# Weight streams of a two-block layer: three reduced matmuls on split operands, or one plain 32-bit matmul on the landed weights

## The reference, cut to what matters

```python
# first block
u = rmsnorm(h, attn_norm_w);      z_xbc_q_k_v = u @ w_in          # 2048 x 5184
h = h + mixed @ w_out                                             # 2048 x 2048
v = rmsnorm(h, ffn_norm_w)
h = h + (silu(v @ w_gate) * (v @ w_up)) @ w_down                  # 2048 x 5632, twice; 5632 x 2048
# second block
z = rms_norm(h, g) @ w_in_2                                       # 2048 x 7176
h = h + rms_norm(y @ w_out_2, g)                                  # 2048 x 2048
u = conv3(rms_norm(h, g) @ w_up_2); gate, up = split(u)           # 2048 x 11264
h = h + rms_norm((silu(gate) * up) @ w_down_2, g)                 # 5632 x 2048
h = h + rms_norm((p @ w_ple_proj_2) * sigmoid(rms_norm(h, g) @ w_ple_gate_2), g)
```

## Time and profile before

| | |
|---|---|
| median of 3 runs | 2508.01 us (2504.28 to 2508.35) |
| the profiled execution | 2508.06 us, of which the span is 2506.3 us |
| mean granted clock of PE | 0.994 of full speed |
| busy: PE, DVE, ACT | 2473.7, 1455.4 and 1251.8 us |
| moved by the transfers | 446.27 MB, 178 GB/s over the span |

### The profile page before, as it was taken

The page is one execution under the profiler, slowest core; times in us unless marked ns, Lnnn a source line. Parts: engine busy times, 40 slices in busy tenths (PEclk is TensorE's granted clock), DMA queues, the critical chain, the costliest instruction groups (busy, mean ns, idle before and its releaser), DMA issues.

```text
span 2506.3 us, 32631 instructions
## 1 busy us (share of the span) xinstructions
PE 2473.7 (99%) x11947; PEld 2067.1 (82%) x11947; DVE 1455.4 (58%) x1732; ACT 1251.8 (50%) x1604; POOL 44.9 (2%) x103
## 2 busy tenths in 40 slices
PE   8999999999999999999999999999999999999997
PEld 7888878888888888888888888878888888888886
DVE  6479665545445454445566566566666666544465
ACT  5357744444444444444654355456556555444464
POOL 2300000000000000000000000000000000000000
PEclk9999999999999999999999999999999999999999
DMA  7543445666666666555654555555565656665554
GB/s 254 175 134 113 135 136 184 191 187 191 186 191 188 189 192 202 192 192 178 171 175 135 151 143 177 186 158 183 186 185 183 190 178 189 199 200 193 193 194 142
DMA packets 234754, 446.27 MB, mean 178 GB/s; under 512 B 14288, under 2 KB 31012, under 8 KB 234144
## 3 DMA queue, kind: packets, MB, share of 16 engines
q1 hardware_dynamic: 231920, 434.83, 56.2%
q0 software_dynamic: 2736, 10.10, 1.3%
HBM read 442.78 MB, written 2.10 MB: 178 GB/s over the span
## 4 chain that ended last, share of the span: by engine, by line
PE 96%; DVE 2%; ACT 1%; issue 0%; DMA 0%; SPq 0%; DVEq 0%; ACTq 0%
PE pg L2191 26%; PE pg L2193 26%; PE pg L2192 26%; PE pg L2250 3%; PE pg L2251 3%; PE pg L2252 3%; PE pt L2851 1%; DVE wlo L1347 1%; PE pt L2666 1%; PE pt L2262 1%; PE pt L2370 1%; PE pt L2435 1%; PE pt L2461 1%; PE pt L2448 0%; PE pt L2649 0%
## 5 line engine op out<-in xcount | busy, mean ns | idle before, releaser
L1347 DVE TENSOR_TENSOR wlo<-raw,whi 128x1024 fp32r<-128x1024 f32 (+3 forms) x844 | 1004.9, 1197 | 980.4 <-ACT whi L653 978.7
L653 ACT ACTIVATE whi<-raw 128x1024 fp32r<-128x1024 f32 (+3 forms) x844 | 871.8, 1036 | 1164.1 <-PE pg L2193 1048.5
L2191 PE MATMUL pg<-whi,AH 128*128 128x512 f32 (+1 forms) x1920 | 749.5, 390 | 5.1 <-DVE AL L1486 3.0
L2193 PE MATMUL pg<-whi,AL 128*128 128x512 f32 (+1 forms) x1920 | 742.8, 387 | 0.0
L2192 PE MATMUL pg<-wlo,AH 128*128 128x512 f32 (+1 forms) x1920 | 742.1, 387 | 0.0
L2191 PEld LDWEIGHTS pg<-whi,AH 128*128 128x128 f32 x1920 | 362.1, 189 | 77.1 <-DVE AL L1486 3.4
L2193 PEld LDWEIGHTS pg<-whi,AL 128*128 128x128 f32 x1920 | 361.6, 188 | 73.7
L2192 PEld LDWEIGHTS pg<-wlo,AH 128*128 128x128 f32 x1920 | 362.3, 189 | 70.8
L2191 PE MATMUL pg<-whi,FH 128*128 128x512 f32 x696 | 271.3, 390 | 0.0
L2193 PE MATMUL pg<-whi,FL 128*128 128x512 f32 x696 | 270.8, 389 | 0.0
L2192 PE MATMUL pg<-wlo,FH 128*128 128x512 f32 x696 | 270.8, 389 | 0.0
(11 more groups left out here) (477 smaller groups left out, 2033.1 us busy)
## 6 DMA issues: line engine op xcount, KB each, us to landing
raw<-w_up SPq DMA_DIRECT2D x264, 512.0 KB, 3.8
raw<-w_down SPq DMA_DIRECT2D x176, 512.0 KB, 3.6
raw<-w_in SPq DMA_DIRECT2D x152, 512.0 KB, 3.6
raw<-w_gate SPq DMA_DIRECT2D x88, 512.0 KB, 3.6
raw<-w_out SPq DMA_DIRECT2D x64, 512.0 KB, 3.6
raw<-w_ple_gate SPq DMA_DIRECT2D x32, 512.0 KB, 4.5
raw<-w_in SPq DMA_DIRECT2D x32, 388.0 KB, 3.2
raw<-w_in SPq DMA_DIRECT2D x16, 280.0 KB, 3.0
```

What stands on the lines that cost most here:

```text
L653: A(whi[:, n % RING, 0:w], raw[:, n % RING, 0:w], ACT.Copy).then_inc(hi_ready, 1)
L1347: V.tensor_tensor(wlo[:, n % RING, 0:w], raw[:, n % RING, 0:w], whi[:, n % RING, 0:w].bitcast(F32), ALU.subtract).then_inc(lo_ready, 1)
L2191: mm(o, xh, wh, start=first and k == 0, stop=False)
L2193: ins = mm(o, xl, wh, start=False, stop=last and k == SK - 1)
```

## The change

Each unit becomes one matmul of `F32` operands: a tile of activations `x` and the landed weights in `raw`. The rounded copies and the rests, of weights and of operands, are gone, with the semaphores between ACT and DVE that they needed. The ring `raw` has eight steps. PE waits for the landing itself, and SP for PE's `step_used` of eight steps before.

```diff
-RING = 4
+RING = 8
...
-                        sp.wait_ge(lo_ready, n - RING + 1 + d)
+                        sp.wait_ge(step_used, n - RING + 1 + d)
...
-                A(whi[:, n % RING, 0:w], raw[:, n % RING, 0:w], ACT.Copy).then_inc(hi_ready, 1)
...
-                V.tensor_tensor(wlo[:, n % RING, 0:w], raw[:, n % RING, 0:w], whi[:, n % RING, 0:w].bitcast(F32),
-                                ALU.subtract).then_inc(lo_ready, 1)
...
+            def landed(n, d=0):
+
+                pe.wait_ge(raw_landed[n % RING], 16 * (n // RING + 1) + d * (16 // RING))
...
+                landed(n, d)
                 for k in range(SK):
-                    wh = whi[:, n % RING, k * w:(k + 1) * w]
-                    wl = wlo[:, n % RING, k * w:(k + 1) * w]
                     for t in range(NT):
-                        mm(o, xh, wh, start=first and k == 0, stop=False)
-                        mm(o, xh, wl, start=False, stop=False)
-                        ins = mm(o, xl, wh, start=False, stop=last and k == SK - 1)
+                        ins = mm(pg[:, b + t, 0:w], x[:, kt0 + k, t * P:(t + 1) * P], raw[:, n % RING, k * w:(k + 1) * w],
+                                 start=first and k == 0, stop=last and k == SK - 1)
```

The activations need one copy out of `pt` now instead of a copy and a subtraction. The turned tiles come in groups of two; ACT copies the even groups and DVE the odd ones, each with the scale as before (`prep` on both engines, semaphores `even_ready` and `odd_ready`):

```diff
-                for g in (2 * c, 2 * c + 1):
-                    act.wait_ge(turned, quarters(p) + g + 1)
...
-                        ins = A(hi[:, kt - kt0, :], src[:, k, :], ACT.Copy, scale=sc)
-                    ins.then_inc(a_hi, 1)
+                g = 2 * c
+                act.wait_ge(turned, quarters(p) + g + 1)
...
+                        ins = A(dst[:, 2 * g + k - kt0, :], src[:, k, :], ACT.Copy, scale=VT[:, w:w + 1])
+                ins.then_inc(even_ready, 1)
...
+                g = 2 * c + 1
+                dve.wait_ge(turned, quarters(p) + g + 1)
...
+                        ins = V.tensor_scalar(dst[:, 2 * g + k - kt0, :], src[:, k, :], VT[:, w:w + 1], None, ALU.mult)
+                ins.then_inc(odd_ready, 1)
```

More of the change, by code:

```diff
@@ L643, in link, with stream @@
                 act.wait_ge(act_chain, chain[0])
[L645 to L652, removed]
-                A(whi[:, n % RING, 0:w], raw[:, n % RING, 0:w], ACT.Copy).then_inc(hi_ready, 1)
[L655 to L678, removed]
+            def stream(g, evac, between):
+                for c in range(len(g["chunks"])):
+                    for j in range(g["S"]):
+                        between.get((c, j), no)()
+                    evac(c, 0, g["N"] + (c + 1) * g["S"])
             def evac_copy(dst, g, scale=1.0):
@@ L1004, in down, with f1_copy @@
                         between.get((c, j), no)()
-                        split(N + c * S_ + RING + j)
                     evac(c, 0, N + (c + 1) * S_)
             F1, F2 = G["ffn1"], G["ffn2"]
-            def f1_hi(c, d):
+            def f1_copy(c, d):
                 act.wait_ge(f_turned, c + d)
-                A(FH[:, ds((d + c - 1) * 4, 4), :], pt[:, 0:2, :].rearrange("p b (c n) -> p (b c) n", n=TOK), ACT.Copy)\
-                    .then_inc(f_hi, 1)
+                A(FT[:, ds((d + c - 1) * 4, 4), :], pt[:, 0:2, :].rearrange("p b (c n) -> p (b c) n", n=TOK), ACT.Copy)\
+                    .then_inc(f_ready, 1)
             def f1_silu(c, d):
@@ L1180, in _ @@
                     evac_in1(n // 8)
-                split(RING + n)
-            f1_in = lambda c: lambda: prep(2, lambda k: V_FFN + k, AH, c)
+            f1_in = lambda c: lambda: prep(2, lambda k: V_FFN + k, XA, c)
             if upto < 8: return
@@ L1214, in _ @@
             between.update({at_step(fox_start(u) + 1): lambda u=u: fox(u) for u in range(10)})
-            stream(G["in2"], evac_copy(Z2, G["in2"], SM[:, 4:5]), between, loop=False)
+            stream(G["in2"], evac_copy(Z2, G["in2"], SM[:, 4:5]), between)
             if upto < 13: return
@@ L1220, in _ @@
                 between.get(i, no)()
-                split(G["out2"]["N"] + RING + i)
                 if i in HALF_ENDS:
@@ L1236, in _, with p_copy2 @@
             f2_in(0)()
-            split(F2["N"] + 2)
             f2_in(1)()
-            split(F2["N"] + 3)
             if upto < 17: return
-            ffn(F2, [after(f2_up), after(f2_conv_up), lambda c, d: (f2_gate(c, d), after(f2_hi)(c, d)), f2_conv_gate],
+            ffn(F2, [after(f2_up), after(f2_conv_up), f2_gate, f2_conv_gate],
                 {2: f2_in(2), 4: f2_in(3), 6: norm_ffn2})
-            def p_parts():
+            def p_copy2():
                 act.wait_ge(p_tr, 1)
-                A(PH[:], pt[:, 3, :].rearrange("p (k n) -> p k n", k=2), ACT.Copy).then_inc(p_hi, 1)
+                A(XP[:], pt[:, 3, :].rearrange("p (k n) -> p k n", k=2), ACT.Copy).then_inc(p_ready, 1)
             g = G["down2"]
@@ L1311, in _ @@
                     between.get((c, j), no)()
-                    split(g["N"] + c * 8 + RING + j)
                 if c == 0:
@@ L1339, in link, with stream @@
                 dve.wait_ge(dve_chain, chain[0])
-            def split(n, d=0, w=None):
-                if n >= NSTEP:
-                    return
-                w = SK * (w or WIDTH[n])
-                dve.wait_ge(hi_ready, n + 1 + d)
-                V.tensor_tensor(wlo[:, n % RING, 0:w], raw[:, n % RING, 0:w], whi[:, n % RING, 0:w].bitcast(F32),
-                                ALU.subtract).then_inc(lo_ready, 1)
-            def stream(g, evac, between={}, loop=True):
-                S_, N, n = g["S"], g["N"], len(g["chunks"])
-                def one(c, dc, dn):
-                    for j in range(S_):
-                        if isinstance(dc, int):
-                            between.get((c, j), no)()
-                        split(N + c * S_ + RING + j, dn)
-                    evac(c, dc, N + (c + 1) * S_ + dn)
-                for c in range(2):
-                    one(c, 0, 0)
-                loops = uniform_pairs(g)
-                if loops > 2 and loop:
-                    with dve.Fori(0, loops - 1) as i:
-                        for c in (2, 3):
-                            one(c, i * 2, i * (2 * S_))
-                    done = 2 * loops
-                else:
-                    done = 2
-                for c in range(done, n):
-                    one(c, 0, 0)
+            def stream(g, evac, between):
+                for c in range(len(g["chunks"])):
+                    for j in range(g["S"]):
+                        between.get((c, j), no)()
+                    evac(c, 0, g["N"] + (c + 1) * g["S"])
             def evac_copy(dst, g, scaled=False):
@@ L1728, in side @@
                     s = unit_step(u)
-                    if n == s + 7 and UNITS[u][0]:
-                        o_low(u)
                     if n == s:
@@ L2075, in _ @@
             between.update({at_step(fox_start(u)): lambda u=u: fox(u) for u in range(10)})
-            stream(G["in2"], evac_copy(Z2, G["in2"], True), between, loop=False)
+            stream(G["in2"], evac_copy(Z2, G["in2"], True), between)
             if upto < 13: return
@@ L2204, in chunk, with halved @@
                         before(j)
-                    step(g["N"] + c * g["S"] + j, dn, 2 * (C_ % 2), SK * j, w, j == 0, j == g["S"] - 1, hi, lo)
-            def halved(g, hi, lo, c, j0, j1, n0, first, before):
+                    step(g["N"] + c * g["S"] + j, dn, 2 * (C_ % 2), SK * j, w, j == 0, j == g["S"] - 1, x)
+            def halved(g, x, c, j0, j1, n0, first, before):
                 C_ = g["C"] + c
@@ L2213, in halved, with last_two @@
                     before(j)
-                    step(g["N"] + n0 + j, 0, 2 * (C_ % 2), SK * (j % 4), CW, j == first, j == (first + 7) % 8, hi[j // 4], lo[j // 4])
-            def last_two(n, b, kt0, hi, lo):
+                    step(g["N"] + n0 + j, 0, 2 * (C_ % 2), SK * (j % 4), CW, j == first, j == (first + 7) % 8, x[j // 4])
+            def last_two(n, b, kt0, x):
                 for t in range(NT):
-                    o = pg[:, b + t, :]
                     for i in range(2):
                         if t == 0:
-                            pe.wait_ge(lo_ready, n + i + 1)
+                            landed(n + i)
                         for k in range(SK):
-                            wh = whi[:, (n + i) % RING, k * CW:(k + 1) * CW]
-                            wl = wlo[:, (n + i) % RING, k * CW:(k + 1) * CW]
-                            xh = hi[:, kt0 + SK * i + k, t * P:(t + 1) * P]
-                            xl = lo[:, kt0 + SK * i + k, t * P:(t + 1) * P]
-                            mm(o, xh, wh, start=False, stop=False)
-                            mm(o, xh, wl, start=False, stop=False)
-                            ins = mm(o, xl, wh, start=False, stop=i == 1 and k == SK - 1)
+                            ins = mm(pg[:, b + t, :], x[:, kt0 + SK * i + k, t * P:(t + 1) * P], raw[:, (n + i) % RING, k * CW:(k + 1) * CW],
+                                     start=False, stop=i == 1 and k == SK - 1)
                     if t == 0:
@@ L2269, in mix2_tiles, with first @@
```

(65 more changed lines are left out.)

248 lines of the change are left out of this document (76 added, 172 removed).

## The result

The changed kernel takes 3070.33 us in the median (3068.28 to 3070.57, 4 runs) against 2506.15 us before (2502.61 to 2508.35, 4 runs): a ratio of 1.225, 95% interval 1.223 to 1.227. The forecast was 3088 us and 3060 to 3120. The profiled execution took 3068.28 us, with a span of 3066.5 us, 560.2 us more than before.

A forecast was written before the change was run, and what follows sets the result against it. PE was taken to bound the kernel through the number and length of its matmuls. 2506.3 + 587 for plain units - 7 for waits gave a 3086 us span, so a median of 3088 us, range 3060 to 3120.

The forecast's parts named there:

- What bounds the kernel: Whole kernel: PE, busy 2473.7 of 2506.3 us; shortening only DVE or ACT can gain at most PE's 32.6 idle us.
- the split is free: Weight split on DVE (1004.9 us) and ACT (871.8 us): removal priced at nothing, because PE covers it, except where PE waited.
- A plain matmul has two records and four runs over the columns: Stream units after the change: two profile records of 0.430 us per plain matmul, some 6750 records on the new lines.
- the unit of two runs' worth of time: Rival for the stream's units: a plain matmul takes one record, 0.430 us, giving about 1674 us; chance 3%.
- The price of 0.860 us: Cost of a plain 512-column matmul, read from `states` and `y_off`, against 0.681 us for a unit before.
- the bound from above, 0.881: Upper limit for a plain 512-column matmul, from two 256-column matmuls of `hidden` at 0.441 us each.
- the dearer unit: Rival for long rows of plain matmuls: each costs 0.881 us as `hidden` shows, giving 3154 us; chance 7%.
- The landings and the ring: Weight transfers: PE's added wait for landings priced at nothing, 152 GB/s needed; rival of landings as bound 3540 us, 4%.
- The sum: Whole kernel: 2506.3 us plus 587 for the units minus 7 for waits, a span of 3086 us.
- the 3120 wide units: Units of 512 columns in the stream: from 0.681 to 0.860 us each, +558.5 us.
- The narrow ones: Units of 388, 280 and 260 columns: +16.4, +6 and +6 us.
- Idle time of PE: Waits of PE that hang on the split, 7.7 us in all: 7 us of them taken as saved.

The follow-up runs named there:

- e4: Kernel before without DVE's half of the weight split, PE taking the rounded weights in place of their rest, still three matmuls a unit; 2495.51 us, ratio 0.9956.
- e1: Kernel before with two reduced matmuls a unit instead of three, the product of the operand's rest with the rounded weights left out; 1944.67 us.
- e2: Kernel before with a fourth reduced matmul a unit, the product of both rests; 3238.06 us.
- e5: Changed kernel with each 512-column matmul issued as two of 256 columns; 3081.58 us, ratio 1.230 to the kernel before.
- e3: Changed kernel with a ring of four steps instead of eight, two late quarters of x loaded after the first four loads; 3067.12 us, ratio 1.224 to before.
- e6: Kernel before with all rounded copies and rests in bfloat16 instead of the reduced 32-bit type, still three matmuls a unit; 2394.73 us, ratio 0.9553.

## Why the prediction was right, point by point

**What bounds the kernel, and that the split is free.** Right: DVE and ACT fell to 14% and 12%, and PE stayed at 99%. e4 shows it for DVE's half: 1005 us of work removed, 11 us gained, some of them from the clock. ACT's half was removed only together with it, in the change itself. e1 shows how near the limit lay.

**A plain matmul has two records and four runs over the columns.** Right: 6752 records on the four new lines (5968, 704, 48 and 32), forecast some 6750, 0.429 us apart. This rules out the unit of two runs' worth of time. e2 shows that four reduced matmuls are no cheaper than a plain one. Whether a record of a plain matmul runs over its columns twice, or once at half the pace, no run here tells apart; the price is that of two runs either way, and the forecast needs no more.

**The price of 0.860 us.** Right, 0.858 measured, and the bound from above, 0.881, was too careful. e5 has matmuls of 256 columns at 0.2157 us a record, so the dearer unit is out as well; what makes `hidden` dear wasn't tried. Its place among reduced matmuls is not the reason, since in the changed kernel, where none is left, the same sixteen matmuls take the same 7.05 us:

```profile
107.72 7.05 PE pt L2200 x32
```

**The landings and the ring.** Right: no wait, 151 GB/s where 152 was forecast, and e3 with half the ring runs the same.

**The sum.** It gave a span of 3086 us, and 3066.5 came, 19.7 us less. By its own terms: the 3120 wide units cost (55.81 - 44.44) / 64 = 0.1777 us more each, 554.3 instead of 558.5 us: 4.2. The narrow ones cost, against the 0.529, 0.39 and 0.36 us that the earlier trace rows give, 128 x 0.124 + 64 x 0.082 + 64 x 0.079 = 26.2 instead of 28.4: 2.2. Idle time of PE fell by 9.2 us instead of 7: 2.2. And there is a term that the sum lacked: the clock. The prediction read it at 1.00 in the steady stage and put what it might give back at nothing. The traced execution of before lost some 3.2 us near 340 and 3.5 near 1330 us to the level of 1.2 GHz, and the changed kernel is at 1.00 at both places:

```profile
360.00:410.00 50.00, 49.18 (x163) 25.51 (x162) 13.08 (x17) 6.65 (x8) 0.00 (x0) 1.00 0.35 116
1590.00:1640.00 50.00, 50.00 (x189) 28.05 (x188) 11.27 (x10) 6.92 (x7) 0.00 (x0) 1.00 0.42 123
1960.00:2000.00 40.00, 36.76 (x86) 16.74 (x85) 6.14 (x17) 5.26 (x13) 0.00 (x0) 0.91 0.43 131
```

That makes 6.7 more, 15.3 in all. The other 4.4 us I haven't located. The errors of the terms all point the same way, so none of them hid another.

What stays open is why the clock fell. Near 340 us PE waited 0.8 us for no other engine ("issue") in the kernel before, in e4, in e6 and after the change. The clock fell there before and in e6, and stayed at 1.00 in e4 and after the change. Near 1330 us the wait for DVE is gone with the split, and so is the fall. The wait of 3.2 us behind the norm stands in all of them; the clock fell there before, in e4 and after the change (the last window above), and not in e5. So the length of one wait doesn't tell in these runs whether the clock falls. The windows of e6 and of e5:

```profile
310.00:350.00 40.00, 38.05 (x177) 20.09 (x179) 24.23 (x28) 16.07 (x18) 0.00 (x0) 0.91 0.36 119
```

```profile
1960.00:2060.00 100.00, 96.56 (x466) 84.62 (x465) 17.59 (x44) 14.49 (x29) 0.00 (x0) 1.00 0.48 140
```

## What to carry to other kernels

Before taking a plain 32-bit matmul for one run over its columns, count its records against the loop that issues it, and read the distance between them in the chain of work, not their durations: here the side work of the old kernel had the whole answer, to 0.002 us a unit. Removing 1000 us from an engine that is hardly on the path gives back the waits at the seams, here some 6 us of PE's idle time. Time added to every matmul of the bound engine shows in full: 22% for the plain matmul at the price of four bare runs, 29% for a fourth reduced matmul (e2). Where three products of split operands will do in precision, the type of the parts is worth trying: bfloat16 parts gave 110 us, but they keep fewer bits of each value, so whether they will do must be decided for each use.

## What the runs showed of the hardware

Reduced 32-bit matmuls of 512 columns stand 226.7 ns apart in a long row, 158 distances in 35.81 us of the kernel before, 13 ns over the bare columns, though their weight loads of 188 ns fit:

```profile
499.97 0.23 PE pg L2193
...
535.78 0.23 PE pg L2192
```

Plain records of 512 and of 256 columns, with loads of the same length, have 2.5 ns over (429.2 and 215.7 ns), and so, to the rounding of its rows, has bfloat16 with loads of 100 ns (217 ns). So the 13 ns are not the length of the load. At the level of 1.2 GHz they vanish: the nine matmuls above stand (1336.15 - 1332.74) / 8 = 0.426 us apart, and the bare 512 columns take 0.427.

The spread between executions goes with this clock. The seven executions of before beside e1 to e4 had mean granted clocks of 0.994 to 0.996 and times of 2508.6 down to 2505.4 us, the longest with the lowest clock.
